# Block products in the last quarter of an MLP input projection, and sums of weight blocks issued at other places

## The reference

```python
h = rms_norm(x, pre_norm_mix)
y = hybrid_mixer(h, w_in, ..., w_branch_att, w_branch_dn, w_out)   # block-sparse attention beside a gated delta rule
x = x + rms_norm(y, post_norm_mix)
h = rms_norm(x, pre_norm_mlp)
y = jnp.square(jax.nn.relu(h @ w_mlp_in)) @ w_mlp_out              # 1024 -> 4096 -> 1024
return x + rms_norm(y, post_norm_mlp)
```

## Time and profile before

| | |
|---|---|
| median of 3 runs | 748.58 us (748.31 to 748.79) |
| profiled execution | 748.65 us, span 747.1 us |
| TensorE's granted clock, mean | 0.998 of full speed |
| busy share of TensorE, VectorE, ScalarE, POOL | 99%, 58%, 52%, 42% |

### The profile page before, as it was taken

The page is one execution under the profiler, slowest core; times in us unless marked ns, Lnnn a source line. Parts: engine busy times, 40 slices in busy tenths (PEclk is TensorE's granted clock), DMA queues, the critical chain, the costliest instruction groups (busy, mean ns, idle before and its releaser), DMA issues.

```text
span 747.1 us, 11902 instructions
## 1 busy us (share of the span) xinstructions
PE 739.8 (99%) x4168; PEld 608.1 (81%) x4168; DVE 436.2 (58%) x651; ACT 389.3 (52%) x632; POOL 317.3 (42%) x296
## 2 busy tenths in 40 slices
PE   9999999999999999999999999999999999999996
PEld 7788778888887878788888988888888888888885
DVE  5896899990444545345974511221221777778795
ACT  6657842268555365635655733332332655565671
POOL 2357894535444754574526454645645000000002
PEclk9999999999999999999999999999999999999999
DMA  9336223446365577266651279789877476654752
GB/s 341 102 93 205 57 77 108 127 128 184 113 156 157 192 174 204 60 159 204 207 183 29 84 244 290 186 269 282 231 238 212 159 222 197 197 186 153 219 174 113
DMA packets 52893, 129.21 MB, mean 173 GB/s; under 512 B 6096, under 2 KB 6512, under 8 KB 50544
## 3 DMA queue, kind: packets, MB, share of 16 engines
q1 hardware_dynamic: 49120, 109.47, 44.7%
q0 software_dynamic: 3392, 18.88, 13.1%
q10 hardware_dynamic: 336, 0.28, 0.1%
...
## 4 chain that ended last, share of the span: by engine, by line
PE 93%; POOL 3%; ACT 2%; DVE 1%; issue 0%; POOLq 0%; ACTq 0%; DVEq 0%
PE bank L758 28%; PE bank L760 27%; PE bank L759 27%; POOL rsq L2158 2%; PE bank L1005 1%; PE bank L1028 1%; PE bank L1015 1%; POOL w_lo L2164 1%; PE bank L969 1%; PE bank L779 1%; PE bank L933 1%; PE bank L785 1%; PE bank L980 1%; PE bank L1037 1%; PE bank L788 0%; PE bank L1067 0%
## 5 line engine op out<-in xcount | busy, mean ns | idle before, releaser
L2164 POOL TENSOR_TENSOR w_lo<-raw,w_hi 128x512 fp32r<-128x512 f32 x169 | 220.0, 1311 | 238.4 <-ACT w_hi L1220 236.6
L1220 ACT ACTIVATE w_hi<-raw 128x512 fp32r<-128x512 f32 (+2 forms) x214 | 144.9, 684 | 156.3 <-PE bank L760 122.6
L758 PE MATMUL bank<-h_hi,w_hi 128*128 128x512 f32 (+1 forms) x528 | 208.5, 395 | 0.2
L759 PE MATMUL bank<-h_lo,w_hi 128*128 128x512 f32 (+1 forms) x528 | 204.2, 387 | 0.0
L760 PE MATMUL bank<-h_hi,w_lo 128*128 128x512 f32 (+1 forms) x528 | 204.1, 387 | 0.0
L758 PEld LDWEIGHTS bank<-h_hi,w_hi 128*128 128x128 f32 x528 | 99.1, 188 | 25.5 <-issue 5.1
L760 PEld LDWEIGHTS bank<-h_hi,w_lo 128*128 128x128 f32 x528 | 99.2, 188 | 20.6
L759 PEld LDWEIGHTS bank<-h_lo,w_hi 128*128 128x128 f32 x528 | 99.3, 188 | 18.7
L1629 DVE SCALAR_TENSOR_TENSOR relu_sb<-bank,rs_row 128x512 f32<-128x512 f32 x32 | 20.6, 686 | 126.0 <-PE bank L760 114.3
L2305 POOL TENSOR_SCALAR ssh<-ssy 128x1 f32<-128x1 f32 x4 | 1.0, 238 | 151.6 <-ACT junk L1600 151.6
L758 PE MATMUL bank<-w_hi,a_hi 128*128 128x512 f32 x120 | 46.8, 390 | 0.0
...
## 6 DMA issues: line engine op xcount, KB each, us to landing
...
```

Of the source, the lines that this page charges most:

```text
L758: pe.matmul(o, s_hi, m_hi, start=start, stop=False, skip_group_check=True)
L759: pe.matmul(o, s_hi, m_lo, start=False, stop=False, skip_group_check=True)
L1220: return a.activation(o, i_, ACT.Copy, scale=scale)
L2164: g.tensor_tensor(w_lo[:, slot, :], raw[:, slot, :], w_hi[:, slot, :].bitcast(F32), ALU.subtract).then_inc(lo_ready, 1)
```

## The change

The first 12 groups of the MLP input stay as they are (`G_PLAIN`). The last 1024 hidden columns (units 168 to 183 before) are made by seven block products of eight: h is cut in halves by features and by tokens, w_mlp_in's quarter in halves by features and by columns. There are two steps, each of 14 units, two for each product in the order q1, q6, q5, q2, q7, q3, q4, and a unit feeds 12 matmuls of 256 columns. q1, q2 and q4 use weight blocks as they are, the others four new sums of blocks (`u_sum`), which are made in DRAM in the mixer (`IN_SUM_AT`, four copies and adds of 1 MB). The sums of blocks of h are made by VectorE in the early groups. In a step, VectorE makes the results from the banks (e1, f, c11, c22, c12, c21, then a relu of 768 columns in `relu_in`), ScalarE copies q1 (`p1`); the low parts of ten units of a step are VectorE's and of four (1, 3, 7, 11) POOL's. The loads use a ring of eight slots.

The sums of w_mlp_out's blocks are issued elsewhere: eight in the mixer in place of six, seven in groups in place of ten, the last in step 1; w_mix_out's sums too. The blocks of h lie over `x_res`, so SP stores x_res to DRAM in groups 2 and 3 (four stores of 512 KB), and POOL's queue loads it back during the down projection, with `pn_mlp`, which SP loaded in the mixer. The squares and relus of the last step stand in `one(1)`. SP's first loads for the down projection are issued in another order.

```diff
-U_M1 = U_OUT + 64
+G_PLAIN = 12
+U_S = U_OUT + 4 * G_PLAIN
+PER_STEP = 14
+RING = 8
+U_M1 = U_S + STEPS_IN * PER_STEP
...
-OUT_SUM_AT = {48: 0, 52: 1, 60: 2, 87: 3}
+OUT_SUM_AT = {55: 0, 61: 1, 70: 2, 85: 3}
-SUM_AT = {61: (0, 0), 65: (1, 0), 73: (2, 0), 74: (0, 1), 78: (1, 1), 86: (2, 1)}
+SUM_AT = {64: (0, 0), 73: (1, 0), 76: (2, 0), 79: (0, 1), 82: (1, 1), 88: (2, 1), 113: (0, 2), 118: (1, 2)}
-SUM_IN = {2: (0, 2), 3: (0, 3), 4: (3, 0), 5: (3, 1), 7: (2, 2), 8: (2, 3), 9: (1, 2), 10: (1, 3), 12: (3, 2), 13: (3, 3)}
+IN_SUM_AT = {48: (0, 0), 51: (1, 0), 58: (2, 0), 68: (3, 0)}
+SUM_IN = {1: (0, 3), 2: (3, 0), 3: (1, 3), 4: (2, 2), 5: (3, 1), 6: (2, 3), 9: (3, 2)}
+IN_PRODUCTS = ("q1", "q6", "q5", "q2", "q7", "q3", "q4")
+IN_BANK = {"q1": 0, "q2": 0, "q6": 2, "q7": 2, "q4": 2, "q5": 4, "q3": 4}
+LOW_POOL = (1, 3, 7, 11)
+LOW_DVE = tuple(v for v in range(PER_STEP) if v not in LOW_POOL)
...
     pn_mix = at("pn_mix", 80, [P, D])
-    pn_mlp = at("pn_mlp", 84, [P, D])
+    pn_mlp = at("pn_mlp", 0, [P, D])
...
+    u_sum = [nc.dram_tensor(f"{name}_in_sum", (2 * STEPS_IN * P, 512), F32).ap() for name in ("v1", "t3", "t2", "t4")]
+    x2_copy = nc.dram_tensor("x2_copy", (NT, P, D), F32).ap()
...
             if u in SUM_AT:
                 q, i = SUM_AT[u]
                 if q == 2:
-                    sp_.wait_ge(t_added[0], 16 * (i + 1))
+                    sp_.wait_ge(*added(0, i + 1))
+                if (q, i) == (2, 0):
+                    sp_.wait_ge(*added(2, 0))
+                    sp_.wait_ge(*added(3, 0))
                 sp_.dma_start(*t_copy(q, i)).then_inc(t_copied[q], 16)
+            if u in IN_SUM_AT:
+                q, chunk = IN_SUM_AT[u]
+                if q == 2:
+                    sp_.wait_ge(t_added[2], 16 * CHUNKS)
+                if q == 3:
+                    sp_.wait_ge(t_added[1], 16 * CHUNKS)
+                sp_.dma_start(*u_copy(q, chunk)).then_inc(t_copied[2 + list(IN_SUM_AT).index(u) % 2], 16)
...
-        for g in range(2, 16):
+        sp_.dma_start(*t_copy(*SUM_IN[1])).then_inc(t_copied[SUM_IN[1][0]], 16)
+        for g in range(2, G_PLAIN):
             for j in range(4):
                 load(0, j, mlp_source(g, j), g * 4 + (U_OUT + j - RAW - 1))
+                if g in (2, 3) and j % 2:
+                    t = 2 * (g - 2) + j // 2
+                    if t == 0:
+                        sp_.wait_ge(*x2_signal(2))
+                        sp_.wait_ge(*x2_signal(3))
+                    sp_.dma_start(x2_copy[t], x_res[:, t, :]).then_inc(copied_out, 16)
             if g in SUM_IN:
                 q, i = SUM_IN[g]
                 if q == 2:
-                    sp_.wait_ge(t_added[0], 16 * N_SUM)
+                    sp_.wait_ge(*added(0, N_SUM))
                 if q == 3:
-                    sp_.wait_ge(t_added[2], 16 * (2 if i < 2 else N_SUM))
+                    sp_.wait_ge(*added(2, 2 if i < 2 else N_SUM))
                 sp_.dma_start(*t_copy(q, i)).then_inc(t_copied[q], 16)
+        for s in range(STEPS_IN):
+            for v in range(PER_STEP):
+                u = U_S + PER_STEP * s + v
+                if v >= RING - RAW or s:
+                    sp_.wait_ge(*low_of(u - RING))
+                sp_.dma_start(raw_of(u), in_source(s, v)).then_inc(raw_signal(u)[0], 16)
+                if (s, v) == (1, 0):
+                    sp_.wait_ge(*added(3, 3))
+                    sp_.dma_start(*t_copy(3, 3)).then_inc(t_copied[3], 16)
         for q in range(3):
-            sp_.wait_ge(t_added[q], 16 * N_SUM)
+            sp_.wait_ge(*added(q, N_SUM))
...
                     sp_.wait_ge(part_lo, before + s + 2)
                 part(s, two_source(i, s))
...
+        def in_product(s, name):
+            if name == "q1":
+                pe.wait_ge(made_in, made("c11", s - 1, 1)) if s else pe.wait_ge(relu_done, 2 * G_PLAIN - 2)
+            elif name == "q6":
+                pe.wait_ge(made_in, made("c21", s - 1, 1)) if s else pe.wait_ge(relu_done, 2 * G_PLAIN)
+            elif name == "q5" and s:
+                pe.wait_ge(made_in, made("c12", s - 1, 1))
+            elif name == "q2":
+                pe.wait_ge(p1_copied, 2 + 2 * s + 2)
+            elif name == "q7":
+                pe.wait_ge(made_in, made("e1", s, 1))
+            elif name == "q3":
+                pe.wait_ge(made_in, made("f", s, 1))
+            elif name == "q4":
+                pe.wait_ge(made_in, made("c22", s, 1))
...
+            for half in range(2):
+                u = U_S + PER_STEP * s + 2 * IN_PRODUCTS.index(name) + half
+                pe.wait_ge(*low_of(u))
+                for kk in range(2):
+                    for e in range(2):
+                        c = slice(kk * 256 + e * P, kk * 256 + e * P + P)
+                        x_ = three(bank[IN_BANK[name] + e][:, 0:256], w_hi[:, u % SPL, c], w_lo[:, u % SPL, c],
+                                   *in_operand(name, 2 * half + kk), name in ("q1", "q6", "q5") and half + kk == 0,
+                                   name in ("q2", "q4", "q3") and half + kk == 2)
+                x_.then_inc(unit_done, 1)
+        for s in range(STEPS_IN):
+            for name in IN_PRODUCTS:
+                in_product(s, name)
...
                     pe.wait_ge(part_lo, i * 8 + (s + 1))
...
+        def mlp_in_step(s):
+            for v in range(PER_STEP):
+                u = U_S + PER_STEP * s + v
+                if u + LEAD < U_M1:
+                    split_in(u + LEAD)
+                else:
+                    a.wait_ge(unit_done, u)
+                    w_split(u + LEAD - U_M1, 1, 16)
+                if v == 2:
+                    if s:
+                        a.wait_ge(made_in, made("c21", s - 1, 1))
+                    for e in range(2):
+                        copy(p1[:, e, :], bank[e][:, 0:256]).then_inc(p1_copied, 1)
+                if s and v in (3, 4):
+                    square_in(s - 1, v - 3)
...
+        def one(i, last=False, ends=False):
             for g in range(4):
+                if ends and g == 2:
+                    for e in range(2):
+                        square_in(STEPS_IN - 1, e)
                 a.wait_ge(part_done, i * 8 + (2 * g + 2 - 8))
...
-        def one(i):
+        def one(i, ends=False):
             for g in range(4):
                 w_low(2 * g, 2, i * 8 + (2 * g + 2))
+                if ends and g < 2:
+                    relu_in(STEPS_IN - 1, g)
                 if g % 2:
                     a_low(i * 2 + g // 2, g // 2, slice(0, 4), i * 2 + (g // 2 + 1))
                 else:
...
+        def c21(s, e):
+            v.tensor_tensor(relu_sb[:, 2 * e + 1, 0:256], bank[2 + e][:, 0:256], p1[:, e, :], ALU.subtract).then_inc(made_in, 1)
+        def relu_in(s, e):
+            v.wait_ge(made_in, made("c21", s, 1))
+            r_ = relu_sb[:, 2 * e:2 * e + 2, :].rearrange("p m c -> p (m c)")[:, 256:]
+            stt(r_, r_, 0.0, rs_ext[:], ALU.max, ALU.mult).then_inc(made_in, 1)
+        def step_in(s):
+            for v_ in range(PER_STEP):
+                u = U_S + PER_STEP * s + v_
+                if v_ == 0 and s:
+                    v.wait_ge(unit_done, u)
+                    for e in range(2):
+                        c21(s - 1, e)
+                if v_ == 1 and s:
+                    for e in range(2):
+                        relu_in(s - 1, e)
+                if v_ == 4:
+                    v.wait_ge(unit_done, u)
+                    v.wait_ge(p1_copied, 2 + 2 * s + 2)
+                    for e in range(2):
+                        v.tensor_tensor(e1[:, e, :], p1[:, e, :], bank[2 + e][:, 0:256], ALU.subtract).then_inc(made_in, 1)
+                if v_ == 6:
+                    v.wait_ge(unit_done, u)
+                    for e in range(2):
+                        v.tensor_tensor(f1[:, e, :], p1[:, e, :], bank[4 + e][:, 0:256], ALU.add).then_inc(made_in, 1)
+                if v_ == 8:
+                    v.wait_ge(unit_done, u)
+                    for e in range(2):
+                        v.wait_ge(act_ready, 2 * (G_PLAIN - 2 + 2 * s + e) + 2)
+                        stt(relu_sb[:, 2 * e, 0:256], bank[e][:, 0:256], 0.0, rs_row[:, 0:256], ALU.max, ALU.mult).then_inc(made_in, 1)
+                if v_ == 10:
+                    v.wait_ge(unit_done, u)
+                    v.wait_ge(made_in, made("f", s, 1))
+                    for e in range(2):
+                        v.tensor_tensor(relu_sb[:, 2 * e + 1, 256:512], bank[2 + e][:, 0:256], f1[:, e, :], ALU.subtract).then_inc(made_in, 1)
+                if v_ == 12:
+                    v.wait_ge(unit_done, u)
+                    for e in range(2):
+                        v.tensor_tensor(relu_sb[:, 2 * e, 256:512], bank[4 + e][:, 0:256], e1[:, e, :], ALU.add).then_inc(made_in, 1)
+                in_low(u + LEAD)
+                if v_ in (7, 9):
+                    combine_in(G_PLAIN - 2 + 2 * s + v_ // 2 - 3)
...
+        v.wait_ge(late_in, 16 * (NT + 1))
...
         g.wait_ge(mlo_ready, 4)
```

(116 more changed lines are left out.)

182 lines of the change are left out of this document (138 added, 44 removed).

## The result

| kernel | median, us | runs | range, us |
|---|---|---|---|
| before | 748.52 | 17 | 748.31 to 749.53 |
| changed | 751.46 | 17 | 748.32 to 757.04 |

The ratio is 1.0033 (95% interval 1.0019 to 1.0046): 0.33% slower, where 746.7 was forecast with a range of 745.1 to 749.6. The scatter is a result too: the runs of the kernel before lie within 1.2 us, those of the changed one within 8.7.

What follows compares the result with a forecast made beforehand. TensorE, busy 99% of the span, was taken as the bound. Terms of -3.3 + 0.9 + 0.1 + 0.4 = -1.9 us gave 746.7 us, with a range of 745.1 to 749.6.

Steps and rivals of the forecast that it cites:

- The matmuls: MLP input's last quarter: 336 matmuls of 256 columns replace 192 of 512, 40.2 us for 43.5, 3.3 us less.
- The fourth rival: New steps: TensorE restarts 14 times at 0.1 each, 1.4 us more, 748.1; chance 0.20 together with the second rival.
- The copy at 113: w_mix_out's last units: a 1 MB copy delays loads 114 and 115, 0.9 us more (0.15 to 1.95).
- Start of step 0: First new step: the fourth unit's low part waits behind POOL's split, 0.1 us more (0 to 0.5).
- Inside a step: New steps: VectorE has 17.2 us of work in 20.1, its tightest result 0.9 us early, so 0 cost.
- the rival in which VectorE becomes the bound: New steps: POOL splits hold VectorE up for their full length, 4.6 us in all, 751.3; chance 0.10.
- Second pass: Down projection's `one(1)`: moved relus delay a_lo by 1.2 us against 0.75 in hand, 0.4 us more.
- Sums and copies hidden in the groups: MLP groups: four added stores offset by three fewer sums, taken as 0, at most 4.7 us.
- the second rival: MLP groups 2 to 6: stores make loads late by 1 to 3 us, 747.1 to 749.6; chance 0.20 with the fourth rival.

Runs made afterwards that it cites:

- squares_fitted: Changed kernel with group sums issued later, the copy at 113 moved behind load 116, and second-pass relus and squares reordered: 745.52 us, ratio 0.9956.
- spread_116: Changed kernel with group sums issued later, the copy at 113 moved behind load 116 and its add behind split 118: 747.29 us, ratio 0.9982.
- only_116: Changed kernel with only the copy at 113 moved behind load 116, its add left in place: 750.68 us, ratio 1.0030.
- experiment 7: Changed kernel with later group sums, moved copy and reordered second pass, POOL making seven units' low parts per step, not four: 746.75 us, against 746.70 with four.
- packed_again: squares_fitted with the group sums back where the change puts them (groups 1 to 6 and 9): 747.84 us, ratio 0.9993.
- experiment 6: The run packed_again: squares_fitted with the changed kernel's placement of the group sums: 747.84 us against 745.52.
- again_timed: Changed kernel unaltered, timed a second time beside the kernel before: 749.99 us, ratio 1.0015.

## Why the prediction was wrong

- **The matmuls: right.** 40.2 us forecast from the pitch of the earlier trace rows, 40.31 measured, in every profile; `squares_fitted` gets the whole 3.1 us. The fourth rival, restarts of 0.1 at each product, would have made 41.6.
- **The copy at 113: right, in size too.** 0.9 forecast, 0.15 to 1.95; the five profiles with the copy there show 0.87, 0.70, 0.44, 1.04 and 1.18, and none of those without it has the gap. In the medians it shows less plainly: `spread_116` gained 0.5, `only_116` nothing.
- **Start of step 0: right within its bounds.** 0.1 forecast, no gap seen.
- **Inside a step: right.** TensorE lost no time to VectorE, and the rival in which VectorE becomes the bound fell: the steps are dense in the changed kernel, with VectorE busy for 31.95 of 40.31 us, and stay so in experiment 7. The Trainium skill ("SBUF — State Buffer", section "Who interferes with whom") states that a VectorE instruction with two SBUF inputs contends with a GpSimd instruction that reads SBUF; experiment 7 agrees, with 2.09 us for a relu beside a split against 0.95 alone.
- **Second pass: right in mechanism, too small.** 0.4 forecast, 0.52 to 1.36 measured. The relu was 0.95, with 1.0 taken. In the changed kernel's profile a_lo ended 11.62 us after the down projection's first matmul, against 10.13 before: 1.5 more, where 1.2 was forecast. What the term missed is that VectorE's queue begins later against TensorE there: ScalarE's splits ahead of it stood for loads of the weight sums (2.07 and 0.56 us in that profile, 1.62 in `spread_116`), which before was not so, and a low part that VectorE made 1.85 us ahead of that first matmul now begins 0.44 us behind it. I had costed only what was added to the queue.

```profile
585.73 1.19 ACT L1378 ACTIVATE w_hi<-raw 128x512 fp32r<-128x512 f32 x2 [1.62 <-DMA raw<-t_sum]
```

- **Sums and copies hidden in the groups: the step that failed.** "As w_mlp_out's sums in the groups go from ten to seven ... I take 0." Seven are fewer than ten, but six of them stand in groups 1 to 6 in a row, with the 2 MB of stores, where before groups 2 to 5 had four. And the earlier trace rows is not the stretch of the stores: SP issues them at 428 to 442 in the changed kernel, and its 455 to 466 come behind that. From 435 to 446 the share was 0.62 before and is 1.01 now, ahead of a stretch that was full already. The count was of the whole stage; what counts here is each stretch. The runs put the price at 2.3 us (`packed_again` against `squares_fitted`), up to 5 in single runs. It is the second rival's mechanism and place, and its 1 to 3 us hold that 2.3; it had a chance of 0.20, together with the fourth. Its upper end of 749.6 lies below both medians of the changed kernel (749.99 and 751.46): the second-pass term was short by 0.4 as well, and some 0.6 and 2 us beyond that no run explains.

The sum in retrospect, with the mean gap of five profiles for 113, that of seven for the second pass, and experiment 6 for the groups: -3.2 + 0.85 + 0.8 + 2.3 = +0.75, against +1.3 in `again_timed` and +2.9 in the first 17 runs. The losses need not be independent (a late load may give later ones time to catch up); no run shows it. Why one execution loses 0.6 us in the groups and another 2.5, and why the first timing lay 1.5 above the second, stays open.
